# Last output-projection block tile by tile, and routing steps as fused per-tile VectorE operations

## The reference

```
h = rms_norm(x, norm_mix_w)
x = x + merged(h) @ w_out                       # last projection of the mixer
h = rms_norm(x, norm_ffn_w)
group_prob = softmax(h @ w_group + b_group)      # 4 groups, top 1
e_logits   = h @ w_expert_router + b_expert      # 32 experts, 8 to a group
top-2 experts of the chosen group, weights = g_w * softmax(top 2 logits)
x = x + sum over the two experts of (silu(h @ w_gate[e]) * (h @ w_up[e])) @ w_down[e]
out = rms_norm(x, norm_final_w)
```

## Time and profile before

| | |
|---|---|
| runs | 1023.42, 1023.49, 1024.78 us, median 1023.49 |
| profiled execution | 1022.9 us, its span 1021.0 us, so 1.9 us lie around the span |
| busy in the span | PE 996.3 us (98%), DVE 500.1 (49%), ACT 323.9 (32%), POOL 120.8 (12%) |
| granted TensorE clock | 0.996 of 2.4 GHz |
| DMA | 269.28 MB, mean 264 GB/s, up to 420 GB/s in the expert stage |
| mixer until | about 534.7 us, experts from 561.3 us to the end |

### The profile page before, as it was taken

The page is one execution under the profiler, slowest core; times in us unless marked ns, Lnnn a source line. Parts: engine busy times, 40 slices in busy tenths (PEclk is TensorE's granted clock), DMA queues, the critical chain, the costliest instruction groups (busy, mean ns, idle before and its releaser), DMA issues.

```text
span 1021.0 us, 13126 instructions
## 1 busy us (share of the span) xinstructions
PE 996.3 (98%) x4917; PEld 644.4 (63%) x4917; DVE 500.1 (49%) x810; ACT 323.9 (32%) x531; POOL 120.8 (12%) x152
## 2 busy tenths in 40 slices
PE   8999999999999999999998999999999999999896
PEld 7888788889889988888885333333333333333332
DVE  6268646597778677735525123333223233332235
ACT  6344535586556557622213100000000000000012
POOL 0683077000000000000000000000000000000000
PEclk9999999999999999999999999999999999999999
DMA  9223231344334525162988899999999999999993
GB/s 331 83 83 126 92 114 21 83 125 145 66 91 113 185 42 205 43 213 90 422 307 357 348 420 420 420 420 420 420 420 420 421 420 420 420 421 421 421 414 146
DMA packets 63125, 269.28 MB, mean 264 GB/s; under 512 B 9488, under 2 KB 9680, under 8 KB 38360
## 3 DMA queue, kind: packets, MB, share of 16 engines
q1 hardware_dynamic: 57464, 257.32, 63.6%
q0 software_dynamic: 5344, 11.02, 4.9%
q10 hardware_dynamic: 256, 0.10, 0.0%
HBM read 268.41 MB, written 4.20 MB: 267 GB/s over the span
## 4 chain that ended last, share of the span: by engine, by line
PE 72%; SPq 17%; DVE 5%; DMA 3%; ACT 2%; issue 1%; DVEq 0%; ACTq 0%
PE pj L674 23%; PE pj L854 18%; PE pj L956 12%; SPq L575 11%; PE pj L982 6%; SPq L572 6%; PE cb L631 3%; DMA raw_moe<-in_w_up_dram 3%; PE cb L992 2%; PE cb L993 1%; DVE mkT L1758 1%; DVE wl L1494 1%; PE cb L723 1%; PE cb L695 1%; ACT wh L1136 1%
## 5 line engine op out<-in xcount | busy, mean ns | idle before, releaser
L956 PE MATMUL pj<-raw_moe,xT 128*64 128x512 f32 x1016 | 227.6, 595 | 4.2 <-DMA raw_moe<-in_w_up_dram 2.4
L1494 DVE TENSOR_TENSOR wl<-raw_mix,wh 128x1024 fp32r<-128x1024 f32 x116 | 146.2, 1262 | 130.9 <-ACT wh L1136 130.6
L1970 DVE TENSOR_TENSOR x<-x,cb 128x512 f32<-128x512 f32 x120 | 77.0, 683 | 190.2 <-PE cb L993 190.2
L956 PEld LDWEIGHTS pj<-raw_moe,xT 128*64 128x64 f32 x1016 | 72.1, 137 | 140.8 <-issue 140.8
L1136 ACT ACTIVATE wh<-raw_mix 128x1024 fp32r<-128x1024 f32 x116 | 122.4, 1057 | 111.4 <-PE pj L674 68.5
L982 PE MATMUL pj<-raw_moe,hf 128*64 128x512 f32 x512 | 116.7, 598 | 1.6 <-ACT hf L1440 1.6
L982 PEld LDWEIGHTS pj<-raw_moe,hf 128*64 128x64 f32 x512 | 34.6, 136 | 67.2 <-issue 67.0
L1445 ACT ACTIVATE yh<-pj,now 128x512 fp32r<-128x512 f32 x32 | 20.4, 683 | 157.6 <-PE cb L993 143.6
L1440 ACT ACTIVATE hf<-cb 128x512 f32<-128x512 f32 x16 | 9.6, 598 | 146.3 <-PE cb L631 146.3
L992 PE MATMUL cb<-yh,hot 128*128 128x512 f32 x124 | 55.2, 445 | 0.0
L674 PE MATMUL pj<-wh,hTh 128*128 128x512 f32 x128 | 50.8, 397 | 1.7 <-DVE hTl L1525 0.7
(11 more groups left out here) (397 smaller groups left out, 1858.5 us busy)
## 6 DMA issues: line engine op xcount, KB each, us to landing
raw_moe<-in_w_gate_dram SPq DMA_DIRECT2D x64, 1024.0 KB, 26.7
raw_moe<-in_w_down_dram SPq DMA_DIRECT2D x64, 1024.0 KB, 26.7
raw_moe<-in_w_up_dram SPq DMA_DIRECT2D x63, 1024.0 KB, 26.0
raw_mix<-in_w_in_dram SPq DMA_DIRECT2D x31, 1024.0 KB, 5.3
raw_mix<-in_w_in_dram POOLq DMA_DIRECT2D x10, 512.0 KB, 5.8
raw_mix<-in_w_ret_branch_dram SPq DMA_DIRECT2D x4, 1024.0 KB, 5.8
raw_mix<-in_w_mlstm_branch_dram SPq DMA_DIRECT2D x4, 1024.0 KB, 5.5
raw_mix<-in_w_out_dram SPq DMA_DIRECT2D x4, 1024.0 KB, 5.1
```

The costliest lines, as they stand in the source:

```text
L956: mm = nc.tensor.matmul(pj[a * CAP:(a + 1) * CAP, up, :], xT[:, 4 * half + k, a * CAP:(a + 1) * CAP], weights_of(m + a)[:, k, :], start=ha ...
L1494: V.tensor_tensor(wl[:, q % RING, :, :], entry_source(q), wh[:, q % RING, :, :].bitcast(F32), ALU.subtract).then_inc(wl_ok, 1)
L1970: V.tensor_tensor(part, part, cb[:, 2 + g % 2, :], ALU.add).then_inc(c_add, 1)
```

## The change

The last block (21) leaves `mix_half`: `stream_tile(i)` runs all four entries of one token tile. Transposes of tiles already added to x2 are put between: tile 0, tile 1, turn 0, tile 2, turn 1, tile 3 (with `logits(0)` in its middle), turn 2, `logit_rows(0)`, turn 3, `logits(1)`, `logit_rows(1)`. VectorE and ScalarE follow this order; the scaling of the router weights moves behind the last `wl` entry. The x2 stores of tiles 0 to 2 are issued ahead of chunks 11, 12, 15 and 17, which stay ahead of tile 3's. In the routing, two operations over all four tiles (compare and multiply, or scale and add) become four `scalar_tensor_tensor` operations of one tile each, whose scalar is a [128, 1] column, with one own-wait behind the four. The two subtractions that feed ScalarE's exponentials move behind `hot16`.

```diff
--- before.py
+++ after.py
@@ -596,10 +596,11 @@
             sp.wait_ge(wl_ok, ENTRIES)
             moe_chunk(9, 0, False)
             moe_chunk(10, 0, False)
-            sp.wait_ge(*entry_used(ENTRIES - 3))
-            for m in (11, 12, 15, 17):
-                moe_chunk(m, 0, False)
             for t in range(TT):
+                if t == TT - 1:
+                    sp.wait_ge(*entry_used(ENTRIES - 3))
+                    for m in (11, 12, 15, 17):
+                        moe_chunk(m, 0, False)
                 sp.wait_ge(free[t], free_of(t, BLOCKS - 1))
                 sp.dma_start(x_dram[t * P:(t + 1) * P, :], x2[:, t, :]).then_inc(st_in, 16)
             for m in (16, 18, 19, 20):
@@ -878,12 +879,12 @@
                                 ml_scores(i + 1)
                         for n in TURNS.get((p, u, s), ()):
                             turn_out(n)
-            for b in range(B_WR, BLOCKS):
+            for b in range(B_WR, BLOCKS - 1):
                 block_of(b)
 
-
             def turn_stream(t):
-                pe.wait_ge(free[t], free_of(t, BLOCKS - 1))
+                for i in (0, 1, t) if t == 2 else (t,):
+                    pe.wait_ge(free[i], free_of(i, BLOCKS - 1))
                 for half in range(2):
                     bank = cb[:, 2 * t + half, :] if t < 2 else pj[:, 2 * t + half - TT, :]
                     for k in range(4):
@@ -909,13 +910,40 @@
                     m = nc.tensor.matmul(cb[:, 2, t * 36:(t + 1) * 36], lgT[:, t * P:(t + 1) * P], fold[:, 0:36], start=True, stop=True)
                 m.then_inc(lg_ps, 1)
 
+            def stream_tile(i):
+
+                b = BLOCKS - 1
+                pe.wait_ge(free[i], free_of(i, b - 1))
+                cols = slice(i * P, (i + 1) * P)
+                for j in range(4):
+                    q = entry(b, j)
+                    if i == 0:
+                        pe.wait_ge(wl_ok, q + 1)
+                    for kk in range(2):
+                        k = 2 * j + kk
+                        ops = ((mrgTh[:, k, cols], wh[:, q % RING, kk, :]), (mrgTl[:, k, cols], wh[:, q % RING, kk, :]),
+                               (mrgTh[:, k, cols], wl[:, q % RING, kk, :]))
+                        for n, (lhsT, rhs) in enumerate(ops):
+                            m = nc.tensor.matmul(pj[:, i, :], lhsT, rhs, start=k == 0 and n == 0, stop=k == KD - 1 and n == 2)
+                    if j == 3:
+                        m.then_inc(full[i], 1)
+                    elif i == 3:
+                        m.then_inc(pair_used, 1)
+                    if i == 3 and j == 1:
+                        pe.wait_ge(wrt_ok, 1)
+                        logits(0)
+
+            stream_tile(0)
+            stream_tile(1)
             pe.wait_ge(tr_l, 2 * KD)
-            for t in range(TT):
-                turn_stream(t)
-            pe.wait_ge(wrt_ok, 1)
-            logits(0)
+            turn_stream(0)
+            stream_tile(2)
+            turn_stream(1)
+            stream_tile(3)
+            turn_stream(2)
+            logit_rows(0)
+            turn_stream(3)
             logits(1)
-            logit_rows(0)
             logit_rows(1)
 
             def stay_awake(n):
@@ -1411,18 +1439,21 @@
                 bank = cb[:, 2 * t + 1, :] if t < 2 else pj[:, 2 * t + 1 - TT, :]
                 nc.scalar.activation(h2T[:, 4:8, t * P:(t + 1) * P], bank.rearrange("p (k n) -> p k n", k=4), ACT.Copy).then_inc(h2T_a, 1)
 
+            def logits_copy(u):
+                act.wait_ge(lgT_ps, 2 * u + 2)
+                nc.scalar.activation(lgT[:, 256 * u:256 * (u + 1)], cb[:, u, 256 * u:256 * (u + 1)], ACT.Copy).then_inc(lgT_ok, 1)
+
             square(0)
             square(1)
             stream_copy(0)
+            stream_copy(1)
             square(2)
-            stream_copy(1)
+            logits_copy(0)
             stream_copy(2)
             square(3)
             stream_copy(3)
             root(5, TT)
-            for u in range(2):
-                act.wait_ge(lgT_ps, 2 * u + 2)
-                nc.scalar.activation(lgT[:, 256 * u:256 * (u + 1)], cb[:, u, 256 * u:256 * (u + 1)], ACT.Copy).then_inc(lgT_ok, 1)
+            logits_copy(1)
             nc.scalar.activation(xg[:, :], onesq[:, 0:1].to_broadcast([P, D]), ACT.Copy, scale=0.0).then_inc(zero_ok, 1)
             act.wait_ge(e1_in, 1)
             nc.scalar.activation(rt[:, 5, 0:TT * NG], rt[:, 5, 0:TT * NG], ACT.Exp).then_inc(e1_ok, 1)
@@ -1681,7 +1712,7 @@
                             dve.wait_ge(gs_ok, 18)
                         dve.wait_ge(full[i], full_of(i, p))
                         V.tensor_tensor(sgm[:, ct, :], pj[:, i, :], sgm[:, ct, :], ALU.mult).then_inc(free[i], 1)
-                    if p in (B_WO, B_WO + 1):
+                    if p == B_WO:
 
                         half = slice(512 * (p - B_WO), 512 * (p - B_WO + 1))
                         if p == B_WO and i == 0:
@@ -1714,12 +1745,6 @@
                     own(V.tensor_copy(before16[:, :], kc[:, K_BEFORE:K_BEFORE + P]))
                     own(V.tensor_copy(prio[:, :], kc[:, K_PRIO:K_PRIO + NE]))
                     V.tensor_copy(iot[:, :], kc[:, K_SLOT:K_SLOT + CAP]).then_inc(it_ok, 1)
-                if b == B_WO + 1:
-
-                    dve.wait_ge(br_in, 128)
-                    V.tensor_tensor(wrt[:, :, 0:36], wrt[:, :, 0:36], nwc[:, :].unsqueeze(2).to_broadcast([P, KD, 36]), ALU.mult)
-                    V.memset(wrt[:, :, 36:HALF], 0.0)
-                    V.tensor_tensor(fold[:, :], kc[:, K_IDENT:K_IDENT + HALF], kc[:, K_IDENT + HALF:K_IDENT + P], ALU.add).then_inc(wrt_ok, 1)
                 if b == B_MQ:
 
                     dve.wait_ge(grow_a, 4)
@@ -1887,13 +1912,27 @@
             for b in range(B_WR, BLOCKS):
                 evict_block(b - 1)
                 block_of(b)
-            evict_block(BLOCKS - 1)
-
-
-            for t in range(TT):
+            def stream_sum(t):
+                dve.wait_ge(full[t], full_of(t, BLOCKS - 1))
+                V.tensor_tensor(x2[:, t, 512:D], pj[:, t, :], x2[:, t, 512:D], ALU.add).then_inc(free[t], 1)
+
+            def stream_turned(t):
                 dve.wait_ge(h2T_ps, 2 * t + 1)
                 bank = cb[:, 2 * t, :] if t < 2 else pj[:, 2 * t - TT, :]
                 V.tensor_copy(h2T[:, 0:4, t * P:(t + 1) * P], bank.rearrange("p (k n) -> p k n", k=4)).then_inc(h2T_v, 1)
+
+            dve.wait_ge(br_in, 128)
+            V.tensor_tensor(wrt[:, :, 0:36], wrt[:, :, 0:36], nwc[:, :].unsqueeze(2).to_broadcast([P, KD, 36]), ALU.mult)
+            V.memset(wrt[:, :, 36:HALF], 0.0)
+            V.tensor_tensor(fold[:, :], kc[:, K_IDENT:K_IDENT + HALF], kc[:, K_IDENT + HALF:K_IDENT + P], ALU.add).then_inc(wrt_ok, 1)
+            stream_sum(0)
+            stream_sum(1)
+            stream_turned(0)
+            stream_sum(2)
+            stream_turned(1)
+            stream_sum(3)
+            stream_turned(2)
+            stream_turned(3)
             dve.wait_ge(sq_ok, 4 * TT)
             rstd(5, ssq[:, 0:TT], TT, D)
             dve.wait_ge(lg_ps, 2)
@@ -1905,18 +1944,18 @@
             def first_best(score, best, n, a_, b_):
 
                 x_, y_ = tiles(a_, n), rt[:, b_, 0:TT]
-                own(V.tensor_tensor(x_, score, best.unsqueeze(2).to_broadcast([P, TT, n]), ALU.is_equal))
-                own(V.tensor_tensor(x_, x_, prio[:, NE - n:NE].unsqueeze(1).to_broadcast([P, TT, n]), ALU.mult))
+                for t in range(TT):
+                    m = V.scalar_tensor_tensor(x_[:, t, :], score[:, t, :], best[:, t:t + 1], prio[:, NE - n:NE], ALU.is_equal, ALU.mult)
+                own(m)
                 own(V.reduce_max(y_, x_, AX.X))
                 own(V.tensor_tensor(x_, x_, y_.unsqueeze(2).to_broadcast([P, TT, n]), ALU.is_equal))
 
-            own(V.tensor_tensor(lg[:, :, :], cb[:, 2, 0:TT * 36].rearrange("p (t n) -> p t n", n=36),
-                                stat[:, 2, 0:TT].unsqueeze(2).to_broadcast([P, TT, 36]), ALU.mult))
-            own(V.tensor_tensor(lg[:, :, :], lg[:, :, :], brt[:, :].unsqueeze(1).to_broadcast([P, TT, 36]), ALU.add))
+            for t in range(TT):
+                m = V.scalar_tensor_tensor(lg[:, t, :], cb[:, 2, t * 36:(t + 1) * 36], stat[:, 2, t:t + 1], brt[:, :], ALU.mult, ALU.add)
+            own(m)
             gl, el = lg[:, :, 0:NG], lg[:, :, NG:36]
             gmax = rt[:, 7, 0:TT]
             own(V.reduce_max(gmax, gl, AX.X))
-            V.tensor_tensor(tiles(5, NG), gl, gmax.unsqueeze(2).to_broadcast([P, TT, NG]), ALU.subtract).then_inc(e1_in, 1)
             first_best(gl, gmax, NG, 3, 4)
 
             own(V.tensor_scalar(tiles(3, NG), tiles(3, NG), -1.0, BIG, ALU.add, ALU.mult))
@@ -1927,9 +1966,10 @@
             first_best(el, m1, NE, 1, 4)
             own(V.scalar_tensor_tensor(el, tiles(1, NE), -2 * BIG, el, ALU.mult, ALU.add))
             own(V.reduce_max(m2, el, AX.X))
-            V.tensor_tensor(rt[:, 6, 0:TT], m2, m1, ALU.subtract).then_inc(e2_in, 1)
```

(2 more changed lines are left out.)

## The result

| | before | after |
|---|---|---|
| median | 1023.37 us (6 runs) | 1029.73 us (6 runs) |
| ratio, 95% interval | | 1.006, 1.0047 to 1.0073 |
| profiled execution | 1022.9 | 1029.65 |
| its span | 1021.0 | 1027.8 |

The change makes the kernel 6.4 us slower, between the forecast 5.1 us and the end of the range. PE and VectorE do the same work as before (997.1 us busy against 996.3, 500.5 against 500.1): the loss is waiting, and all of it lies in the 60 us from the start of the last block (512.99) to the restart of the weight stream, which is the issue of chunk 24 (572.07).

The account below looks back on a forecast made before the run. The expert stage was taken as bound by its DMA stream, whose start waits for pair 0's first chunks. Terms 1.3 + 0.3 + 2.7 + 0.8 = 5.1 us gave a median of 1028.6 us, range 1024.9 to 1030.8.

Parts of the forecast that it names:

- routing starts later: After the last block's logits: first VectorE routing operation at 544.70 instead of 543.42, 1.3 us later.
- fused operations less moved ones: VectorE routing: four-operation forms cost +0.5 us, the two moved subtractions save 0.18, net +0.3.
- gather issued later: Gather of tokens after the routing: issued at 555.7 instead of 554.13, 1.6 us later.
- transposes later: PE's transposes of gathered tokens: start about 564.2 instead of 559.9, +4.3 us, 1.6 from routing and 2.7 from the gather.
- clock dip: PE idles waiting for the gather, then runs at a lower clock: 0.8 us, between nothing and 1.3.
- chunk 24, and so the end: Restart of the weight stream: chunk 24 issued at 570.6, 5.1 us later, and the end equally later.
- The turns: Last block's new tile order: nothing saved on PE, one exposed stretch, `logits(1)` starting at 541.65 instead of 541.0.
- The transfers: Chunks 11, 12, 15, 17 issued at 533.9, ten microseconds later; queue full until 563.3, gather taking 8.3 us, not 4.7.
- The stream: Expert stage's weight transfers: a gap remains before the restart; the rest starts 5.1 us later and ends so.
- The gather is not held up: Rival at the gather: it lands in less than 5.8 us, only 1.6 us remain, 1025.1; chance 0.14.
- Faster: Rival in the routing: cheap fused operations and no clock fall at 552 leave less PE idling, 1022.4; chance 0.03.

Follow-up runs that it names:

- The late chunks alone: Kernel before with one edit: SP issues the x2 stores of tiles 0 to 2 ahead of chunks 11, 12, 15 and 17; 1026.84 us, ratio 1.0033.
- the run with the gap filled: Changed kernel with five filler matmuls instead of two between the slot table and the transposes of the gathered tokens; 1028.13 us, ratio 1.0055 against the kernel before.

## Why the prediction was right

The place, the mechanism and the order of the terms were right; the sum was 1.5 us short in the trace and 1.1 in the median. By its own steps:

| step | predicted | measured |
|---|---|---|
| routing starts later | 1.3 | 545.33 - 543.42 = 1.9 |
| fused operations less moved ones | 0.3 | (551.72 - 545.33) - (549.40 - 543.42) = 0.4 |
| gather issued later | 1.6 | 556.26 - 554.13 = 2.1 |
| transposes later | 4.3 | 564.91 - 559.92 = 5.0 |
| clock dip | 0.8 | 5.57 - 4.21 = 1.4, and 0.2 longer transposes |
| chunk 24, and so the end | 5.1 | 572.07 - 565.48 = 6.6 |

- **The turns.** Tile 3 ended at 538.89, not 538.45: behind a switch between kinds of matmul a piece takes a tenth or two longer (a tile right behind a turn 5.50 instead of 5.44, the half tile behind the logits 2.96 instead of 2.72, `logits` 1.88 and 1.97 instead of 1.80). The exposed wait was there, but it ended at 542.15 instead of the predicted 541.65. That 0.5 and the 0.17 of the longer `logits(1)` make up the 0.6 us missing here. Putting the copy first won back only 0.2 us: it is the copy, not the square.
- **The gather's issue.** 1.9 + 0.4 is 2.3, and it came 2.1 later. From `hot16` to the gather it is 4.54 us, before 4.73. In the profile before, that stretch had PE at 0.50; the token table's 16 matmul records took 0.60 us there and 0.47 here.
- **The fused operations.** 0.74 us for four of 32 elements, predicted 0.73 from the row with column scalars. The Trainium skill's statement on this (VectorE: DVE Perf Modes, "The DRAIN you can't avoid") would have had four at about 1 us, an estimate of 4 x 0.25; the trace does not bear it out. The same section says that a next operation that is not held starts earlier, and the four here start 0.16 apart. It was right to cost them at a loss; in time alone they cannot be told from no change.
- **The transfers.** Issue predicted at 533.9, seen at 534.09; the queue full until past 560, seen above 400 GB/s until 562.5; the gather 8.3, seen 8.5. The late chunks alone bring 3.5 us, and the gather lands in 4.4 us with the queue dry. The way from the late chunks' trace to the changed kernel's adds up too: chunk 24 is 572.07 - 569.10 = 3.0 us later, of which the gather's issue is 1.95, its longer way 8.51 - 7.68 = 0.8, and what lies between landing and chunk 24 0.2. The Trainium skill's rule that the engines alternate between queues (DMA: Bandwidth & Descriptors, "Queues, rings and completion order") fits a gather that lands while 416 GB/s go on; how they alternate no run here shows.
- **The clock.** Mis-sized by almost half: I took 0.8 between nothing and 1.3; it was 1.4, a full dip, since it fell wholly behind the gap, on the first gate matmuls. The 0.8 was a guess between bounds, so the mechanism was foreseen and its size was not. The transposes of the gathered tokens took 0.73 us instead of 0.48 before; they did so at a clock of 1.00 too, in the run with the gap filled, so that 0.25 is not the dip. That a wait for DMA brings the clock down is also what the Trainium skill says (TensorE: Matmul & The Clock Gate, "HAM oscillation — how this bites in real kernels"), and the trace agrees, at 0.65 to 0.66 of full for 5 us.
- **The stream.** Its later part did not change by more than 0.2 us: 6.6 at its restart, 6.75 at the end. The run with two chunks held back shows that the quiet stretch before the restart was needed: with early chunks still moving in it, the stream is late by itself.
- **The rivals.** "The gather is not held up" was made true by the held chunks, and then the gather path is 1.2 us late, where 1.6 was the price. "Faster" needed the routing's dip to go and nothing else to be late. The dip did go in the profile after, but it only made PE wait longer for the gather, 3.7 us where 2.7 were predicted.

What stays open: how much of the 6.4 us in the timed runs is a change in the dips of the routing itself. The profiles compared are one of each, and the one after has no dip there, the one before has. The forecast was made against that one profile, and where the dips of other executions lie could not be read from it.

## What to carry to other kernels

When work is put in another order, list the semaphores that transfers wait on before counting the compute engines: here a wait "entry used by all tiles" moved by ten microseconds, and the price came 20 us later, on a small gather that shares the DMA engines with the late bulk. Bulk that is late can delay the latency-critical transfer, or, held back behind it, the stream that follows at full rate: here holding 2 MB back won 2.9 us and left a new wait of 2.3. And four operations with a column scalar on 4 to 36 elements each were no gain over two wide ones, even though they saved a wait.

## What the runs showed of the hardware

- A gather of 0.5 MB through GpSimd's queue took 4.3 to 4.7 us in the six traces in which the other queue was dry or running dry at its issue, and 7.7 to 8.5 us in the five in which it was full. With the late chunks alone it landed at 561.99, in the middle of windows with 431 and 416 GB/s.
- A `scalar_tensor_tensor` of 32 elements with a column scalar started 0.16 us after the one before ((0.74 - 0.25)/3, with 0.25 us for one of them); one of 4 elements 0.13 us after ((0.62 - 0.22)/3).
- The kernel before, unchanged, ran between 1021.85 and 1024.92 us, and its time goes with its mean granted clock, 0.998 to 0.993: a thousandth of mean clock with half a microsecond. The traces show two stretches at 0.50, near 12 us and near 553 us, that come and go from one execution to the next and cost 0.8 to 0.95 and 1.0 us. So differences below 0.2% should be compared at equal clock, and in a trace from a point behind the early dip.
